# Deferring the fourth and fifth norm and widening the products of two down projections in a two-block transformer kernel

## The reference

```python
def conv_ffn(x, ln_g, up_w, conv_w, conv_b, down_w):
    u = causal_dwconv(rms_norm(x, ln_g) @ up_w, conv_w, conv_b)
    gate, up = u[..., :FFN_DIM], u[..., FFN_DIM:]
    return (jax.nn.silu(gate) * up) @ down_w
...
    mod = jnp.dot(c_act, w_ada[l]) + b_ada[l]
    sh1, sc1, ga1, sh2, sc2, ga2 = split(mod, 6)
    xn = rms_norm_2(h, g_mix[l]) * (1.0 + sc1) + sh1          # the fourth norm (n4)
    proj = jnp.dot(xn, w_in[l]) + b_in[l]
    q, k, v, qi, ki, wi, xr, yr, gate_a, gate_b = split(proj)
    attn = dsa_attention(q, k, v, qi, ki, wi, rel_bias)       # scores, top-k, softmax
    ...
    h = h + ga1 * jnp.dot(merged, w_out[l])
    xn = rms_norm_2(h, g_ffn[l]) * (1.0 + sc2) + sh2          # the fifth norm (n5)
    up = causal_dwconv_2(jnp.dot(xn, w_up[l]), conv_ffn_w[l], conv_ffn_b[l])
    val, gte = split(up)
    h = h + ga2 * jnp.dot(silu(gte) * val, w_down[l])
```

## Time and profile before

| | us |
|---|---|
| runs of the kernel before, median of 3 (lowest, highest) | 1148.47 (1147.61, 1148.58) |
| the profiled execution, as timed | 1147.75 |
| span of its trace, first to last instruction | 1146.0 |
| PE busy in it | 1127.0 |
| DVE busy | 922.6 |
| ACT busy | 699.4 |

### The profile page before, as it was taken

The page is one execution under the profiler, slowest core; times in us unless marked ns, Lnnn a source line. Parts: engine busy times, 40 slices in busy tenths (PEclk is TensorE's granted clock), DMA queues, the critical chain, the costliest instruction groups (busy, mean ns, idle before and its releaser), DMA issues.

```text
span 1146.0 us, 24061 instructions
## 1 busy us (share of the span) xinstructions
PE 1127.0 (98%) x9194; PEld 1095.8 (96%) x9194; DVE 922.6 (81%) x1608; ACT 699.4 (61%) x1011; POOL 185.1 (16%) x233
## 2 busy tenths in 40 slices
PE   7999999999999999999999999999999999999997
PEld 6999999999999999999999999999988999999987
DVE  5899887788888878877888877679997769888784
ACT  5767885566665457875766653465876347666531
POOL 1000241011112200000111121101324101333310
PEclk9999999999999999999999999999999999999999
DMA  7465456655557864434555578575353655555570
GB/s 268 168 227 186 173 175 246 229 184 183 183 174 275 294 227 151 139 116 144 193 183 183 174 251 302 188 251 180 121 164 118 241 182 173 179 183 183 184 273 37
DMA packets 43713, 220.22 MB, mean 192 GB/s; under 512 B 8063, under 2 KB 12656, under 8 KB 22640
## 3 DMA queue, kind: packets, MB, share of 16 engines
q1 hardware_dynamic: 31552, 185.25, 46.7%
q0 software_dynamic: 9264, 30.94, 7.3%
q10 hardware_dynamic: 2816, 2.90, 0.8%
HBM read 217.97 MB, written 1.11 MB: 191 GB/s over the span
## 4 chain that ended last, share of the span: by engine, by line
PE 90%; DVE 6%; ACT 2%; issue 1%; DMA 0%; DVEq 0%; ACTq 0%
PE ps L870 77%; PE ps L959 3%; DVE wl L567 2%; PE ps L963 1%; ACT wh L553 1%; PE ps_idle L1029 1%; PE ps_idle L1139 1%; PE ps L1500 1%; DVE work L2277 1%; PE ps L1036 0%; DMA x<-in_x 0%; PE ps L1341 0%; PE ps L1477 0%; DVE work L2255 0%; PE ps L1475 0%
## 5 line engine op out<-in xcount | busy, mean ns | idle before, releaser
L870 PE MATMUL ps<-xh,wl 128*128 128x256 f32 x1776 | 509.3, 287 | 1.8 <-DVE xl L2272 1.1
L870 PE MATMUL ps<-xl,wh 128*128 128x256 f32 x1776 | 502.8, 283 | 0.0
L870 PE MATMUL ps<-xh,wh 128*128 128x256 f32 x1776 | 502.6, 283 | 0.0
L567 DVE TENSOR_TENSOR wl<-raw,wh 128x2048 fp32r<-128x2048 f32 (+1 forms) x175 | 394.6, 2256 | 69.6 <-ACT wh L553 68.9
L553 ACT ACTIVATE wh<-raw 128x2048 fp32r<-128x2048 f32 (+1 forms) x178 | 333.2, 1874 | 89.4 <-PE ps L870 69.8
L870 PEld LDWEIGHTS ps<-xh,wl 128*128 128x128 f32 x1776 | 340.7, 192 | 9.2 <-issue 6.7
L870 PEld LDWEIGHTS ps<-xl,wh 128*128 128x128 f32 x1776 | 340.8, 192 | 0.6 <-issue 0.5
L870 PEld LDWEIGHTS ps<-xh,wh 128*128 128x128 f32 x1776 | 340.7, 192 | 0.0
L870 PE MATMUL ps<-actr,wh 128*128 128x256 f32 x1624 | 293.0, 283 | 0.0
L870 PEld LDWEIGHTS ps<-actr,wh 128*128 128x128 f32 x1624 | 253.2, 192 | 0.0
L870 PE MATMUL ps<-actr,wl 128*128 128x256 f32 x812 | 231.3, 285 | 0.5 <-DVE wl L567 0.5
(11 more groups left out here) (279 smaller groups left out, 1231.7 us busy)
## 6 DMA issues: line engine op xcount, KB each, us to landing
raw<-in_up SPq DMA_DIRECT2D x66, 1024.0 KB, 4.9
ada_w<-in_w_ada POOLq DMA_DIRECT2D x54, 256.0 KB, 4.9
raw<-in_xbc SPq DMA_DIRECT2D x12, 1024.0 KB, 5.1
work<-in_w_ada POOLq DMA_DIRECT2D x42, 256.0 KB, 5.2
raw<-in_z SPq DMA_DIRECT2D x8, 1024.0 KB, 5.0
raw<-in_so SPq DMA_DIRECT2D x8, 1024.0 KB, 5.0
raw<-in_dn0a SPq DMA_DIRECT2D x8, 1024.0 KB, 4.9
raw<-in_dn1a SPq DMA_DIRECT2D x8, 1024.0 KB, 5.2
```

The costliest lines, as they stand in the source:

```text
L567: nc.vector.tensor_tensor(wl[:, b % RING, 0:n], raw[:, b % RING, 0:n], wh[:, b % RING, 0:n].bitcast(F32), ALU.subtract).then_inc(lo_done, 1)
L870: mm = nc.tensor.matmul(o, l, r, start=start and n == 0, stop=stop and n == 2)
```

## The change

1. dn0 and dn1 get the 512-wide products that dn2 has, in their first three groups. DVE adds two halves of each bank.
2. The fourth norm is deferred for the kk slab and the first qi slab. The shift is added as a column: `xh`, `xl` become 258 columns wide, the last two hold the shift (split into halves), so that a tile's bank also gets W*shift in columns 256 and 257. When DVE takes the tile out it adds W*shift to the projection's bias (`early_bias`) and multiplies the rest by the factor (`early`), and ACT adds that bias. Meanwhile DVE and ACT mix the normalised operands `ch`, `cl` for all later slabs (qi1, vw, qb, yr, xr, gates).
3. The fifth norm is deferred in the same way for the first two slabs of up2 (`up_h`, `up_l`, `early_up`); the third slab on uses normalised xh, xl.
4. `norm_sum` with its fill products is replaced at both by `norm_squares` and `norm_factor` inside the second tile. The modulation's steps move: the first under dn1 (slab 1), the second ahead of wor. The w_ada pieces of qi move to qb0 and yr0. POOL waits for eight more low halves ahead of the gates' weights.

```diff
-ADA = {..., "dn1": 11, "kk": 1, "qi": 2, "vw": 1, "woa": 2,
+ADA = {..., "dn1": 11, "kk": 1, "vw": 1, "qb0": 1, "yr0": 1, "woa": 2,
...
-DEFERRED = {"n1": (1, "ffn_ln0"), "n2": (2, "kv_ln"), "n3": (4, "ffn_ln1")}
-HALVED = ("xbc1", "xbc2", "up2+1")
+DEFERRED = {"n1": (1, "ffn_ln0"), "n2": (2, "kv_ln"), "n3": (4, "ffn_ln1"), "n4": (5, "gs1")}
+HALVED = ("xbc1", "xbc2")
...
+            def shifted_tile(name, t, ready=None, ks=range(KD)):
+
+                b, g = PL.S[name], PL.G[name] + t
+                if ks[0] == 0:
                     pe.wait_ge(lo_done, b + 1)
                     acquire(pe, g)
+                for k in ks:
+                    if ready:
+                        ready(k)
+                    off = k * 256 + t * P
+                    mm = mm3(bank(g)[:, 0:T + 2],
+                             (wh[:, b % RING, off:off + P], wl[:, b % RING, off:off + P]),
+                             (xh_wide[:, k, :], xl_wide[:, k, :]), k == 0, k == KD - 1, False)
...
+                    if first_two and isinstance(i, int) and i == 0 and j < 2:
+                        for t in range(2):
+                            acquire(pe, g0 + 2 * j + t)
+                            for k in range(kts):
+                                if j == 0 and t == 0:
+                                    first_two(k)
+                                if j == 0 and t == 1 and k == 2:
+                                    norm_squares("n5", 5)
+                                if j == 0 and t == 1 and k == 6:
+                                    norm_factor("n5", 5)
...
-                        if name == "dn2" and i < 3:
+                        if kind == PAIR3 and i < 3:
...
-            norm_sum("n4", 4)
-            two_slabs(((PL.S["kk"], PL.G["kk"]), (PL.S["qi"], PL.G["qi"])), x_ready(5))
-            slab_tile("qi1", 0)
-            slab_tile("qi1", 1)
+            pe.wait_ge(shift_low, 1)
+            shifted_tile("kk", 0, x_ready(5))
+            shifted_tile("kk", 1, ks=range(0, 2))
+            norm_squares("n4", 4)
+            shifted_tile("kk", 1, ks=range(2, 6))
+            norm_factor("n4", 4)
+            shifted_tile("kk", 1, ks=range(6, 8))
+            shifted_tile("qi", 0)
+            shifted_tile("qi", 1)
+            slab_tile("qi1", 0, (ch, cl), x_ready(6))
+            slab_tile("qi1", 1, (ch, cl))
...
-            ffn(2, "n5", 6, 5)
+            pe.wait_ge(shift_low, 2)
+            stream("up2", (xh, xl), x_ready(8), first_two=x_ready(7))
... ACT
+            for m in range(4):
+                mixed_high(m)
+            hi("qi", 0)
+            for m in range(4, KD):
+                mixed_high(m)
...
             for m in range(KD):
                 if m in (0, 2, 3):
                     hi("wout", max(m - 1, 0))
+                given_back(act, PL.G["wout"] + m)
+                A(up_h[:, m, 0:T], x[:, m, :], ACT.Copy, scale=gain_of("gs2", m)).then_inc(xh_done, 1)
                 square(5, m, PL.G["wout"] + m)
-            ffn(2, "n5", [6], {6: 24}, 5, ("wout", 3))
+                if m == 5:
+                    hi("wout", 3)
+            ffn(2, "n5", [8], {8: 24}, 5, ("up2", 1), first_two=True)
... DVE
                             if scale is None:
+                                if p < 3:
+                                    step.add(V.tensor_tensor(x[:, m, :], bank(g)[:, T:2 * T], x[:, m, :], ALU.add))
+                                    step.wait()
                                 ins = V.tensor_tensor(x[:, m, :], bank(g)[:, 0:T], x[:, m, :], ALU.add)
...
+            ffn(1, "n3", 3, to="n4", between=(1, first_modulation))
+            norm_factor("n4", lambda: split_lo(dve, PL.S["qi1"]))
+            mixed(0)
+            for m in range(1, KD):
+                mixed(m)
+                mixed_low(m - 1)
+            mixed_low(KD - 1)
...
+            early_tile(0, "kk", 0, [(slice(0, 64), vec("b_kk", 0)), (slice(64, P), vec("b_kk", 1))])
+            early_tile(1, "kk", 1, [(every_row, vec("b_ki"))])
+            split_lo(dve, PL.S["vw"])
+            ada("kk", 0)
+            ada("kk", 0)
+            early_tile(2, "qi", 0, [(every_row, vec("b_qi", 0))])
+            early_tile(3, "qi", 1, [(every_row, vec("b_qi", 1))])
+            split_lo(dve, PL.S["qi1"] + LEAD)
+            split_lo(dve, PL.S["vw"] + LEAD)
+            ada("vw", 0)
+            ada("vw", 0)
...
+            def projected_low(m):
+                for n in (m, m + 1):
+                    gained_low(7, "gs2", n, up_h[:, :, 0:T], up_l[:, :, 0:T])
+                for n in (m, m + 1):
+                    accumulate(5, n)
...
+            split_lo(dve, PL.S["up2"] + 1)
+            norm_factor("n5", lambda: split_lo(dve, PL.S["up2"] + 2))
+            second_normed(0)
+            for m in range(1, KD):
+                second_normed(m)
+                second_low(m - 1)
+            second_low(KD - 1)
```

More of the change, by code:

```diff
@@ L334 @@
 PL = make_plan()
-ADA = {"so": 6, "dn0": 11, "v0": 1, "v1": 1, "v2": 1, "v3": 1, "ao": 2, "dn1": 11, "kk": 1, "qi": 2, "vw": 1, "woa": 2,
+ADA = {"so": 6, "dn0": 11, "v0": 1, "v1": 1, "v2": 1, "v3": 1, "ao": 2, "dn1": 11, "kk": 1, "vw": 1, "qb0": 1, "yr0": 1, "woa": 2,
        "dn2": 8}
@@ L977, in stage @@
                         for k in ks:
-                            if ready and (isinstance(i, int) and i == 0 and t == 0 and (first or kind == PAIR3)):
+                            if ready and (isinstance(i, int) and i == 0 and t == 0
+                                          and (first or kind == PAIR3 or (first_two and j == 2))):
                                 ready(k)
@@ L1533, in _ @@
                     head_dots(h + 1)
[L1534 removed]
+                slab_tile(gate_name(h), 1, (ch, cl))
                 if h % 2:
@@ L1834, in constants, with ffn @@
                 A(lam4, lam2, ACT.Exp).then_inc(ea_done, 1)
-            def ffn(f, norm_name, uses, shifts, r, behind, to=None):
+            def ffn(f, norm_name, uses, shifts, r, behind, to=None, first_two=False):
+                if first_two:
+                    split_hi(act, PL.S["up2"] + 2)
                 norm(norm_name, uses, shifts, behind)
@@ L1856, in stage @@
                     if inside(i, j, 0, NF):
+                        if starting and j < 2:
+                            for t in range(2):
+                                given_back(act, tile_group(up, j, t))
+                                A(early_up[:, 2 * j + t, :], early_up[:, 2 * j + t, :], ACT.Identity,
+                                  bias=early_up_bias[:, 2 * j + t:2 * j + t + 1]).then_inc(early_biased, 1)
                         for t in range(2):
-                            if norm_name in DEFERRED:
+                            if starting and j < 2:
+                                act.wait_ge(early_biased, 2 * j + t + 1)
+                                src = early_up[:, 2 * j + t, :]
+                            elif norm_name in DEFERRED:
                                 given_back(act, tile_group(up, j, t), i)
@@ L2344, in residual3 @@
                         lo(name, s)
-                    if between and s == 4:
-                        between()
+                    if between and s == between[0]:
+                        between[1]()
                     if to:
@@ L2704, in stage @@
                                       tile_group(up, j, t))
-                    if inside(i, j, 0, NF):
+                    if inside(i, j, 0, NF) and not starting:
                         split_lo(dve, PL.S[up] + j + LEAD, i)
@@ L2988, in _, with first_modulation @@
-            lo("kk", 0)
-            for s in range(2):
-                lo("qi", s)
-            lo("vw", 0)
+            def first_modulation():
+                modulation(0, 24)
+                V.scalar_tensor_tensor(gs1, mod[:, 8:16], 1.0, vec("g_mix", 0, 8), ALU.add, ALU.mult)\
+                    .then_inc(gain_done, 1)
+                step.add(V.tensor_scalar(vec("b_ga", 0, 16), vec("b_ga", 0, 16), 0.5, None, ALU.mult))
+                step.add(V.tensor_scalar(vec("b_rg", 0, 16), vec("b_rg", 0, 16), 0.5, None, ALU.mult))
+                step.add(V.tensor_scalar(mod[:, 16:24], mod[:, 16:24], 0.5, None, ALU.mult))
+                step.wait()
@@ new lines, in _, with early_tile @@
+            mixed(0)
[3 more added lines that the diff above has]
+            mixed_low(KD - 1)
+            def early_tile(n, name, t, biases):
+                g = PL.G[name] + t
+                wait_tile(dve, name, 0, 0, t)
+                for rows, bias in biases:
+                    V.tensor_tensor(early_bias[rows, n:n + 1], bank(g)[rows, T:T + 1], bias[rows, :], ALU.add)
+                give_back(V.tensor_tensor(early[:, n, :], bank(g)[:, 0:T], rstd, ALU.mult), g)
```

233 lines of the change are left out of this document (146 added, 87 removed).

## The result

The changed kernel takes 1134.95 us (median of 3 runs, 1134.87 to 1135.08) against 1148.47: a ratio of 0.9889 with an interval of 0.9875 to 0.9903. The gain is 13.5 us.

What follows compares the result with a forecast made beforehand. It took TensorE's product count times a 0.120 us pitch, plus holes, as the bound. Terms 1.9 + 4.1 + 2.4 - 0.2 = 8.2 us off 1147.75 or 1148.47 gave 1139.6 or 1140.3, stated as 1139.9; range 1136.3 to 1145.0.

Steps and rivals of the forecast that it cites:

- the time is the number of products times this pitch: Whole kernel: time is the number of products at 0.120 us each, plus the holes.
- rival (d): Slower: 258-wide products run at the plain f32 pitch, costing 18.2 us, time 1158; chance 0.05.
- Wide products: dn0 and dn1: 512-wide products save 0.31 us in each of six groups, 1.9 us.
- Fourth norm: Between dn1 and kk: the 5.77 us hole becomes 1.0, with 0.1 us wait at qi1; gain 4.7 us.
- The selection stage keeps 4.1 of it: Scores to gates: VectorE is saturated, so only its own lead of 4.1 us counts; ends 1.5 and 4.7.
- until 31.7: Ahead of the scores: VectorE's last w_ada wait ends 31.7 us after dn1's end; scores start at 32.3.
- the prediction's own sign of being wrong: First score instruction: forecast wrong if VectorE starts the scores less than 3 us earlier relative to dn1's end.
- Rival (b): Selection stage: VectorE's lead is lost again, fourth norm gives nothing; gain 4.1 us, time 1144.0; chance 0.20.
- Fifth norm: wout into up2: deferral gains 2.4 us after waits of 1.25, 0.25 and 0.7 us; ends 0 and 4.6.
- Two more columns: Eight tiles of 24 products with 258 columns: 192 x 0.9 ns, a cost of 0.2 us.
- At nothing: VectorE's additions in dn0 and dn1, moved modulation steps and POOL's wait for eight more low halves: no cost.
- the range's lower end: Whole kernel: rival (a)'s whole gain of 11.0 us with the lower end of the runs, 1136.3 us.

Runs made afterwards that it cites:

- the four kernels of the last group: Changed kernel plus 64-byte gap ahead of xh: alone 1133.8 us; with triples in all down projections and four w_ada pieces at wor 1128.84, dn0 1127.8, dn1 1126.03.
- the kernel with the gap ahead: Kernel before with two unused gaps, 128 bytes a partition ahead of xh and 64 more ahead of actr: 1130.76 us, ratio 0.9851.
- the first kernel with the pieces at wor: Changed kernel with w_ada pieces of qb0 and yr0 done at wor, second modulation behind wor's last slab: 1136.08 us, ratio 0.9909.

## Why the prediction was wrong

- **The term that was missing** is the largest: some 9 us from the pitch of products that the change doesn't touch. The step that failed is the first: "the time is the number of products times this pitch", with the pitch of the kernel before, 0.120 us, kept for the changed one; rival (d) says why it was kept: "nothing but the width changes". The width of two tensors changes the place of their rows and of all that is allocated behind them. The row with the pitch was read as a property of the product; it was one of the place. The four kernels with gaps or wider rows show this.
- **Wide products,** 1.9 us: right for the kernel it was read from (1.76 measured there), mis-sized in the changed one, where the triples that it replaces had become shorter: 1.1 us by the traces of dn0 and dn1, which is lost again ahead of yr0, and 0.25 by the times, which can't be told from nothing. The rule of the Trainium skill that the prediction weighed (TensorE: Matmul & The Clock Gate, section Back-to-back issue gap) is given there for an isolated product, not for a stream of weight loads and products as here; the prediction left that out. It made the pair 2.5 ns shorter and gave 0.7 us in all, by my estimate; the runs have the pair 7 or 3 ns shorter or 13 longer, by layout. The pitch that follows from it for 256 columns, 256/2.4 + 2.5 = 109 ns, no run here shows: the lowest is 113.3.
- **Fourth norm,** 4.7 us: right. Sums 0.81, factor 0.14, no wait at the first tile, no hole over 0.12 us at qi1, where 0.1 had been put; 4.5 us by the table.
- **The selection stage keeps 4.1 of it:** this step failed; it kept 0.8. The failing part is the last wait for w_ada ahead of the scores, put at "until 31.7" with a landing of 4.9 us, a median over the whole kernel. Here POOL issued at 27.3 us behind dn1's end, where 31.7 - 4.9 = 26.8 had been worked out, but the landing of the first took 7.3 us and the second came 1.4 us behind it, at a DMA share of 0.95 (0.75 in the kernel with wide rows alone at the same time), probably because TensorE's lead brings the yr slabs' loads into the same stretch. The first score instruction came 36.6 us behind dn1's end, not 32.3: 1.1 us earlier than before (37.7), where the prediction's own sign of being wrong was less than 3. That the pieces were the cause is shown by the four kernels that moved them: from kk's start to the end of the gate slabs each takes 153.9 us, the changed kernel 157.6. How much of it is the landing (4.7 us of waiting) and how much the four pieces' own work (0.69 us each), they don't part, and that the yr loads slow the landing is read from the windows and not shown. Rival (b) described this mechanism, and its 4.1 us for the edits is near the 3.8 below; its chance of 0.20 was too low. Its place was wrong: at the last transposes TensorE waits 0.66 us as before, and the time goes ahead of yr0 and at the recurrence's gates.
- **Fifth norm,** 2.4 us: right, 2.1. The wait in the first tile, forecast at 1.25, is 1.35 and 0.25; at the third slab 0.21 instead of 0.25, near the sixth 0.14 instead of 0.7.
- **Two more columns:** 30 products of 258 columns take 3.62 us (718.57 to 722.19), 120.7 ns each; 1.9 ns more than a 256-wide one at the new pitch, 0.36 us in all instead of 0.2.
- **At nothing:** the additions in dn0 and dn1 cost nothing that shows; the one hole in dn0 (0.9 us at its second slab) is 0.8 in the kernel with wide rows alone.

By the spans, the wider rows give 1146.0 - 1136.9 = 9.1 us and the edits 1136.9 - 1133.1 = 3.8, the latter as in the table: 0.9 + 4.5 - 3.7 + 2.1 = 3.8. The forecast of 8.2 for the edits was over twice that; the missing term and the failed step pulled in opposite directions, and the missing one was the larger. The 1134.95 us lie below the range for that reason; the range's lower end has a slip besides, since 1147.61 - 11.0 is 1136.6 and not 1136.3.

## What to carry to other kernels

An edit that changes the size of a tensor changes the place of everything behind it, so compare first the pitch of products that the edit doesn't touch; if it moved, run the old kernel with the same sizes and unused columns before crediting the edit. A landing's price is that of its own stretch (its DMA share, the slabs that the change brings forward), not the kernel's median. Work that an engine does on the side belongs where that engine's own timeline has gaps, and a gain ahead of a saturated stage counts only as far as the saturated engine gets it.

## What the runs showed of the hardware

**The pitch of a float32r product depends on where its moving operand lies.** By the bytes within a partition by which the operand's start is moved against the kernel before (from the sizes in each kernel's allocations), at a granted clock of 1.00:

| rows moved by | ns a product | seen in |
|---|---|---|
| nothing | 120.0 | before, xh and actr |
| 128 | 118.7 | actr behind the gap of 128, and in the kernel with wide rows; xh with the gap ahead |
| 192 or 64 | 113.3 or 117.8 | actr moved by 192 (gaps of 128 and 64, and the four kernels of the last group); xh moved by 64 |
| 96 | 120.0 | actr in the kernel with gaps of 64 and 32 |
| rows of 1032 bytes, places of all kinds | 118.8 on average | xh and xl in the changed kernel |

Moved by 192 or 64, a stretch of products without a break keeps one of its two values to the end: none of the 88 stretches of 40 products or more in these six kernels changes. The value changes only across a break, as in dn0 of the kernel with the gap ahead (96 products at 113.3, a wait, 432 at 117.8), and the same stage can have either in different kernels. What chooses stays open, and so does whether the weights' place counts, which wasn't tried.

Kernels with rows there mostly scatter more from run to run: from the shortest to the longest execution it is 3.2 to 7.3 us in these six, and 0.2 to 3.0 in the other runs above, but for the two with the pieces at wor (5.2); the kernel before had 3.8 in the seven executions beside some of them. Part of this may be the clock and not the pitch: in the kernel with pieces at wor, gap and triples the four executions took 1125.5, 1128.5, 1129.1 and 1132.8 us at mean granted clocks of 0.997, 0.993, 0.995 and 0.989.

**The clock.** Where up2's first tile waited for 0.8 and 1.85 us within 5 us, the granted clock fell to 1.2 GHz and 28 products passed in 5 us instead of 44; after waits of 2.3 and 1.9 us at the same place in the trace of the first kernel with the pieces at wor, and after a single one of 1.35 us in the changed kernel, it stayed at 2.4 GHz. The same waits thus bring a fall in one execution and not in another; what decides stays open. Whether the fill products that the change removes would have prevented it isn't shown: in the kernel with the gap ahead, which still has them at the fourth norm, the granted clock fell there too (a mean of 0.67 in 715 to 720 us). Such falls come and go between kernels and executions and cost time of their own, so a difference of 1 to 3 us between two runs needs a look at the granted clock of both.
